# Where gate passes and a norm's sums stand on TensorE in a fused four-layer kernel: order of work in three helpers

## The reference, cut to what matters

```python
def hybrid_layer(x, ...):                     # first block
    h = rms_norm(x, g_mix)
    z = h @ w_in
    ...
    g_a, g_b, g_c = jnp.split(jax.nn.sigmoid(gate_mix), N_MIXERS, axis=-1)
    x = x + (g_a * o_a + g_b * o_b + g_c * o_c) @ w_out
    h = rms_norm(x, g_ffn)
    x = x + jnp.square(jax.nn.relu(h @ w_ff1)) @ w_ff2
    return x

def second_block(x, c, ...):
    for l in range(DEPTH):
        mod = c @ mod_w[l] + mod_b[l]
        sh1, sc1, g1, sh2, sc2, g2 = ...
        h = _rmsnorm(x, norm1_g[l]) * (1.0 + sc1) + sh1
        x = x + g1 * _mixer(h, ...)
        h = _rmsnorm(x, norm2_g[l]) * (1.0 + sc2) + sh2
        x = x + g2 * _conv_ffn(h, ...)
```

## Time and profile before

| | |
|---|---|
| median of 3 runs | 3451.46 us (3446.51 to 3451.64) |
| profiled execution | 3448.53 us, its span 3446.7 us |
| PE busy | 3379.5 us (98%) |
| DVE, ACT, POOL busy | 2023.4 us (59%), 1437.6 us (42%), 1585.9 us (46%) |
| chain that ended last | PE 83%, DVE 8%, ACT 5% |

### The profile page before, as it was taken

How to read it: one execution, slowest core, us unless ns; L and a number is a source line. 1 busy time by engine, 2 the same in 40 slices (tenths; PEclk the granted TensorE clock), 3 DMA queues, 4 the chain that set the end, 5 groups by cost and what they waited for, 6 DMA issues and landing times.

```text
span 3446.7 us, 44127 instructions
## 1 busy us (share of the span) xinstructions
PE 3379.5 (98%) x15776; PEld 2782.1 (81%) x15776; DVE 2023.4 (59%) x3204; ACT 1437.6 (42%) x2513; POOL 1585.9 (46%) x827
## 2 busy tenths in 40 slices
PE   9999999999999999999999999999999999999998
PEld 7877787888888777878888888888888887888887
DVE  5775666113367756661223676668974676768953
ACT  3256743232333567432323447333333447333332
POOL 3447454444434573544444551445544641435543
PEclk9999999999999999999999999999999999999999
DMA  4311023223232111232343221542344221432322
GB/s 172 105 61 43 32 92 116 90 95 100 95 122 98 56 43 38 92 116 98 102 150 127 74 87 38 176 141 104 131 137 148 68 86 50 173 132 103 134 96 99
DMA packets 96890, 346.65 MB, mean 101 GB/s; under 512 B 12640, under 2 KB 13408, under 8 KB 96096
## 3 DMA queue, kind: packets, MB, share of 16 engines
q1 hardware_dynamic: 96736, 344.62, 29.0%
HBM read 338.15 MB, written 6.29 MB: 100 GB/s over the span
## 4 chain that ended last, share of the span: by engine, by line
PE 83%; DVE 8%; ACT 5%; issue 2%; SPq 1%; DMA 0%; POOL 0%; ACTq 0%; DVEq 0%; POOLq 0%
PE ps L391 42%; PE ps L813 15%; PE ps L1421 4%; PE ps L546 4%; PE ps L402 3%; ACT arena L1294 3%; DVE split L1265 2%; PE ps L1701 2%; PE ps L1201 1%; PE ps L458 1%; PE ps L785 1%; PE ps L1911 1%; PE ps L1224 1%; PE ps L801 1%; DVE ps L1257 1%
## 5 line engine op out<-in xcount | busy, mean ns | idle before, releaser
L314 POOL TENSOR_TENSOR weights_lo<-arena,weights_hi 128x1024 fp32r<-128x1024 f32 x464 | 1180.3, 2545 | 1473.2 <-ACT weights_hi L285 1350.7
L285 ACT ACTIVATE weights_hi<-arena 128x1024 fp32r<-128x1024 f32 x490 | 516.9, 1055 | 624.9 <-PE ps L813 354.8
L391 PE MATMUL ps<-moving_hi,weights_hi 128*128 128x512 f32 x2160 | 541.1, 393 | 3.3 <-ACTq L278 1.8
L391 PE MATMUL ps<-moving_lo,weights_hi 128*128 128x512 f32 x2160 | 536.0, 390 | 0.0
L391 PE MATMUL ps<-moving_hi,weights_lo 128*128 128x512 f32 x2160 | 534.0, 389 | 0.0
L391 PEld LDWEIGHTS ps<-moving_hi,weights_hi 128*128 128x128 f32 x2160 | 402.9, 188 | 90.3 <-ACT weights_hi L285 4.0
L391 PEld LDWEIGHTS ps<-moving_lo,weights_hi 128*128 128x128 f32 x2160 | 405.3, 188 | 84.9 <-issue 1.0
L391 PEld LDWEIGHTS ps<-moving_hi,weights_lo 128*128 128x128 f32 x2160 | 405.3, 188 | 83.4
L335 DVE TENSOR_TENSOR moving_lo<-arena,moving_hi 128x512 fp32r<-128x512 f32 x196 | 205.9, 1102 | 223.2 <-ACT moving_hi L330 223.2
L2717 DVE SCALAR_TENSOR_TENSOR arena<-ps,arena 128x512 f32 x64 | 44.1, 692 | 297.8 <-PE ps L391 272.6
L530 POOL TENSOR_TENSOR weights_lo<-arena,weights_hi 128x512 fp32r<-128x512 f32 x76 | 100.0, 1328 | 255.1 <-ACT weights_hi L285 166.6
(11 more groups left out here) (396 smaller groups left out, 5428.5 us busy)
## 6 DMA issues: line engine op xcount, KB each, us to landing
arena<-wstream SPq DMA_DIRECT2D x532, 512.0 KB, 3.3
arena<-modw SPq DMA_DIRECT2D x64, 512.0 KB, 3.7
arena<-modw_first SPq DMA_DIRECT2D x32, 512.0 KB, 4.0
layer_input<-arena SPq DMA_DIRECT2D x2, 2048.0 KB, 10.3
arena<-layer_input SPq DMA_DIRECT2D x2, 2048.0 KB, 8.0
arena<-xT SPq DMA_DIRECT2D x4, 512.0 KB, 5.4
outT<-arena SPq DMA_DIRECT2D x8, 256.0 KB, 2.1
arena<-con SPq DMA_DIRECT2D x1, 1285.0 KB, 10.3
```

Source lines behind the costliest of these rows:

```text
L285: m.nc.scalar.activation(m.w_hi[:, j % 2, :], slab(m, base + at), ACT.Copy).then_inc(hi_ready, 1)
L314: m.nc.gpsimd.tensor_tensor(m.w_lo[:, j % 2, :], slab(m, base + (j if at is None else at)), m.w_hi[:, j % 2, :].bitcast(F32), ALU.subtract)\
L391: mm = m.nc.tensor.matmul(bank, unit_tile(w, k), a[:, k, :], start=(p == 0 and k == 0), stop=(p == 2 and k == KD - 1))
```

## The change

1. In `first_products`, `middle` goes from ahead of chunk 0's pass on the low tiles to behind it. Both callers that give a `middle` are touched.
2. In `attention_stage`, the last but one entry of `unit_of` becomes NU - 1. In latent attention pass 4 goes from unit 6 to 7, in sparse attention pass 13 from unit 14 to 15; in the second block it was at 15 already.
3. In `attention_stage`, the passes of unit 0 go from behind scores 1 to ahead of them, and for later units the passes stay behind the product, except in the last unit, where they go ahead of it.
4. In `compressed_attention_stage`, pass 4 goes ahead of the transposes of group 0, and each pass behind it stands one place earlier.

Nothing is added or removed: the same instructions are issued on PE in another order, and the other engines' programs are the same.

```diff
@@ -434,12 +434,12 @@
     for n, k in enumerate(order):
         product(1, m.w_hi, a_hi, k, start=(n == 0))
-    if middle:
-        middle(pe)
     for n, k in enumerate(order):
         pe.wait_ge(src_lo, n + 1)
         mm = product(0, m.w_hi, a_lo, k, stop=(n == KD - 1))
     mm.then_inc(chunk_done, 1)
+    if middle:
+        middle(pe)
     for k in order:
         product(1, m.w_hi, a_lo, k)
@@ -1166,7 +1166,7 @@
         inner = 3 * len(gates) - 2
-        unit_of = [-1] + [n * NU // inner for n in range(inner)] + [NU]
+        unit_of = [-1] + [n * NU // inner for n in range(inner - 1)] + [NU - 1, NU]
@@ -1237,12 +1237,17 @@
             score(0)
-            for u in range(NU):
+            passes(0)
+            score(1)
+            turn(0)
+            for u in range(1, NU):
                 if u + 1 < NU:
                     score(u + 1)
-                if u:
                     product(u - 1)
-                passes(u)
+                    passes(u)
+                else:
+                    passes(u)
+                    product(u - 1)
                 turn(u)
             passes(NU)
@@ -2320,7 +2325,7 @@
-            for n in range(2, 4):
+            for n in range(2, 5):
                 if n == 3:
                     pe.wait_ge(*attended.freed(6))
                 fill.product(pe, n)
@@ -2329,7 +2334,7 @@
-                fill.product(pe, 4 + g)
+                fill.product(pe, 5 + g)
             pe.wait_ge(values_placed, 4)
@@ -2337,8 +2342,7 @@
-                fill.product(pe, 6 + pair)
-            fill.product(pe, 10)
+                fill.product(pe, 7 + pair)
             fill.product(pe, 11)
```

## The result

| | before | after |
|---|---|---|
| median, us | 3451.13 (11 runs, 3446.51 to 3454.62) | 3461.30 (11 runs, 3456.36 to 3464.74) |
| ratio | | 1.0032 (95% interval 1.0024 to 1.0040) |
| span of the profiled execution | 3446.7 | 3460.6 |
| forecast | | 3454.6, range 3447 to 3462, "no difference" 0.75 |

The change makes the kernel 10.2 us slower. The forecast was 3.2 us slower, which it called no difference; the time lies in its range, but the loss is three times as large and can be told from no change. Stage by stage the two profiles compare as follows. Each stage is measured between two instructions that both kernels have, so shifts from earlier stages don't enter. A stretch in which a clock of 0.50 is granted is called a fall from here on.

What follows compares the result with a forecast made beforehand. PE, busy 98% of the span, was taken to bound the kernel. Terms -3.6 - 3.8 + 10.5 + 1.7 + 0.8 - 2.4 = +3.2 us on the median 3451.46 gave 3454.6 us, eight in ten from 3447 to 3462.

Steps and rivals of the forecast that it cites:

- "no difference": Whole kernel: measured time within about 0.2% (6.9 us) of no change, 3444.6 to 3458.4 us; chance 0.75.
- Compressed stage, -3.6 us: Compressed attention: pass 4 fills PE's idle ahead of the transposes, ending the stage 1.8 us sooner, twice.
- The other end: Compressed attention: later passes, asking for weights some 2 us earlier, are late by all of that; gain 0.
- Projection, +10.5 us: Second block's output projection: starved pass +2.85 and clock fall 4.0 us per layer, less 3.2; between +2.5 and +15.7.
- Rival 1: Projection's clock falls before the single columns until behind the 16 matmuls, 6.6 us per layer: +8.4, 3459.9 us; 14 in 100.
- Feed-forward's sums, -3.8 us: Feed-forward's norm: low-tile pass ahead of the sums shortens PE's idle, 2.8 to 1.9 us; -1.9 twice, between -2.2 and -5.6.
- I take the middle, -1.9: Feed-forward's norm, per layer: between -2.8 us if the clock stays up and -1.1 if it falls as before.
- First gate pass, latent, +1.7 us: Latent attention's start: the pass delays scores 1 and the ACT and DVE chain by 0.85 us, twice.
- First gate pass, the four others, +0.8 us: Sparse and second-block attention starts: first bank 0.65 us late, second bank moves only 0.2 us, four stages.
- short falls of the clock inside the attentions may come or go as the phases shift, some 1.5 us either way: Inside the attentions: an allowance for scatter of 1.5 us either way, outside the summed terms.
- Last gate pass, -2.4 us: Second block's last attention unit: pass fills idle before the product, 1.2 us earlier, twice; latent and sparse attention unmoved.
- Rival 3: Attention shifts are absorbed, early and late, and the projection's fall lasts as before: +1.5 us, 3453.0 us; 13 in 100.

Runs made afterwards that it cites:

- after_again: The changed kernel profiled once more, nothing altered, for other positions of the clock's falls: 3454.77 us, a single execution.
- proj_only: Kernel before, with only the second block's output projection's sums moved behind the pass on the low tiles: 3460.51 us against 3449.13, ratio 1.0032.
- ffn_only: Kernel before, with only the feed-forward's sums moved behind the pass on the low tiles: 3446.76 us against 3449.13, ratio 0.9994.
- gains_filled: gains, plus the feed-forward's chunk 1 pass with low weights moved ahead of the low tiles: 3436.78 us against the kernel before's 3449.21, ratio 0.9959.
- filled_busy: gains_filled plus four unread matmuls in sparse attention's units without a gate pass: 3433.25 us against the kernel before's 3450.84, ratio 0.9961.
- first_busy: first_pass plus four unread 256-column matmuls where the pass had stood: 3452.43 us against the kernel before's 3449.21, ratio 1.0007.
- first_pass: Kernel before, with only unit 0's gate pass moved ahead of scores 1, in all six attentions: 3458.52 us against 3449.21, ratio 1.0023.
- gains: Kernel before, with only the compressed stage, last gate pass and feed-forward's sums edits: 3444.26 us against 3449.21, ratio 0.9983.

## Why the forecast was right and wrong

**Compressed stage, -3.6 us.** Right: 22.9 to 21.1 us in each layer, -1.8 twice. The other end, passes late by their weights, didn't come.

**Projection, +10.5 us.** Right in mechanism and size. Over the 20 layers of the ten profiles with sums ahead the stage takes 98.5 us in the mean (96.55 to 100.04), over the six of after, after_again and proj_only 103.9 (101.3 to 105.8): +5.4 a layer, where the forecast has 2.85 + 4.0 - 1.6 = 5.25. proj_only alone: +11.4 us. Rival 1's deciding point, a fall within the starved pass, did come in proj_only in both layers, and not in after's layer 0: it is not one or the other but differs from execution to execution. What the forecast put at nothing: the norm 41 us behind the sums also gets longer, 7.2 us in the mean of the eight layers with sums behind, 6.3 in the 20 with sums ahead. The clock falls there in all 28, but for 6.8 us in each of the eight and in only four of the 20, for 3.4 us in the other 16. Why it falls for longer wasn't tried.

**Feed-forward's sums, -3.8 us.** The step that failed is "I take the middle, -1.9". The idle shrank from 2.8 to 1.56 us, and where the fall lasted as long as before the stage got 1.0 us shorter (worked out: 1.1). But the clock fell in seven of the eight layers with the sums behind, and for 6.8 us instead of 3.4 in one (22.50 us); it was spared in one (19.31 us). The mean of the eight is 20.9, -1.0 a layer: **-2.0 us**, ffn_only -2.4. Shortening an idle from 2.8 to 1.6 us, with single columns right behind it, gave the full clock in one layer of eight; filling it gave it in four of four (gains_filled and filled_busy).

**First gate pass, latent, +1.7 us.** Right to 0.05 us in each of twelve such stages: from 50.7 to between 51.53 and 51.58.

**First gate pass, the four others, +0.8 us.** This is the term that was wrong, and the largest piece of the miss. Without falls the shifts are as worked out, +0.2 in sparse and +0.1 in the second block (first_busy). But the step "short falls of the clock inside the attentions may come or go as the phases shift, some 1.5 us either way" took for even scatter what the edit itself brings. The pass had covered PE's time between scores 1 and product 0; without it scores 2 and product 0 stand behind waits, and a fall follows in 12 of 20 stages at about 1.25 us, against 0 of 36. That is 3 us a kernel. I had asked whether the chain through ACT and DVE has room for the pass, and not what PE does with the hole at its old place. Filler in that hole takes the falls away and 6 us with them (first_pass against first_busy), which shows the cause. The size isn't settled: 2.3 + 3 us make 5.3, and first_pass measures 9.3 (1.0014 to 1.0032, 5 to 11 us). Its profiled execution, 3454.5 us, is the lowest of its eleven. The three lowest (to 3455.8 us) were granted 0.989 in the mean, the six highest (3458.5 to 3461.2) 0.986 or 0.987; so the others did have more of the lower clock, but where it stands in them no trace shows. It may be at the sparse attention's units without a pass, where first_pass's profile has four falls and the profile before two, but gains has four there too, and proj_only none.

**Last gate pass, -2.4 us.** Right: 102.45 to 101.13 us in gains, 1.3 twice; nothing in latent (50.73 against 50.72) and sparse attention. Rival 3, which had the shifts absorbed, falls with it.

**Sum.** With the sizes the runs show: -3.6 + 1.7 + 0.6 + 3 - 2.6 - 2.0 + 11.4 = +8.5 us against +10.2 (8.3 to 13.8 by the interval). The forecast was +3.2. Of the 7 us between, 3 are the falls at the attentions' starts, 1.8 the feed-forward's clock, 0.9 the projection, the rest within the scatter.

The Trainium skill ("TensorE: Matmul & The Clock Gate", section "HAM oscillation — how this bites in real kernels"), as drawn on in the prediction, tells how a wait between bursts of matmuls, there for a transfer, puts the array back to the slow clock each time. The prediction applied this to the projection alone. The runs agree in direction at two further places, where the waits are for ACT and DVE: attention starts (12 of 20) and the feed-forward (7 of 8); and, the other way round, no fall came there with filler or useful work in the hole (first_busy, gains_filled). They don't agree that it happens each time: the waits are the same to 0.02 us from profile to profile, yet eight of the 20 starts kept the clock, and so did all ten latent ones.

## What to carry to other kernels

Before work is moved into an idle stretch, look at what it leaves behind at its old place: if it covered another engine's work there, the wait returns, and on TensorE a run of waits may also cost the clock, so price it from stages of the same trace that look like that. Then compare several profiles of each kernel, since one profile shows one draw of where the clock falls. A helper's callers must each be costed: here the edit that gains 1 us in one caller loses 5 to 6 in the other, since there the moved sums were the cover. An idle that can't be shortened away is better filled with a pass that has its operands already; that gave 3.6 us a layer where the shorter idle gave 1.0.

## What the runs showed of the hardware that was not expected

The granted clock fell at different places in different executions of the same kernel: the projection of the changed kernel took 101.30 and 104.81 us in one profile and 104.48 and 101.55 in the next, and the eleven runs of each kernel span 8 us (27 runs of the kernel before, 13 us). The shortest falls last 3.4 us (the attentions' first units), proj_only's in the projection 13.7 us. One of 3.4 us cost between 0.9 us (after_again's second-block attention, 102.16 against 101.24) and 1.6 us (the feed-forward with the sums behind, 20.94 against 19.31). Matmuls of one column also ran at half speed there (32 of them 6.7 us instead of 3.5), and they did not keep the clock up: 0.50 was granted behind them in 17 of the 20 layers with the sums ahead.
